# A short-convolution and MLP layer in split float32: in seven of the eight pairs of the up projection the first quadrant is turned over by a transposing DMA of half-word planes instead of by TensorE

## The reference

```python
def reference(x, ...):                      # one layer, kind 0
    h = rmsnorm(x, mix_norm)
    b_gate, c_gate, v = split(h @ w_in, 3)  # 2048 -> 3 x 2048
    y = causal_conv3(c_gate * v)            # per channel, width 3
    x = x + (b_gate * y) @ w_out
    a = relu(rmsnorm(x, mlp_norm) @ w1)     # 2048 -> 8192, the up projection
    return x + (a * a) @ w2                 # 8192 -> 2048, the down projection
```

## Time and profile before

| | us |
|---|---|
| median of three runs | 1909.17 (1907.61 to 1910.26) |
| the profiled execution | 1908.8 |
| its span, first to last instruction | 1907.1 |
| TensorE busy | 1896.7 |
| VectorE busy | 1680.6 |
| ScalarE busy | 1008.1 |
| GpSimd busy | 149.5 |
| read from and written to device memory | 431.01 MB and 93.32 MB |

### The profile page before, as it was taken

The page is one execution under the profiler, slowest core; times in us unless marked ns, Lnnn a source line. Parts: engine busy times, 40 slices in busy tenths (PEclk is TensorE's granted clock), DMA queues, the critical chain, the costliest instruction groups (busy, mean ns, idle before and its releaser), DMA issues.

```text
span 1907.1 us, 22361 instructions
## 1 busy us (share of the span) xinstructions
PE 1896.7 (99%) x8578; PEld 1573.4 (83%) x8578; DVE 1680.6 (88%) x1499; ACT 1008.1 (53%) x1082; POOL 149.5 (8%) x240
## 2 busy tenths in 40 slices
PE   9999999999999999999999999999999999999999
PEld 7888888888888888888888888888888888888887
DVE  6579899898999899988999899998998889888878
ACT  6464564545548476575665756655444343334432
POOL 1100010000011111020111201110000000000000
PEclk9999999999999999999999999999999999999999
DMA  9774768749676966876868768599888878877782
GB/s 380 250 259 127 264 205 325 233 120 330 221 199 276 353 213 205 299 276 210 332 199 307 269 216 323 198 398 399 342 329 345 353 276 314 350 312 281 295 327 116
DMA packets 120282, 525.81 MB, mean 276 GB/s; under 512 B 13040, under 2 KB 17136, under 8 KB 95216
## 3 DMA queue, kind: packets, MB, share of 16 engines
q1 hardware_dynamic: 86336, 401.64, 54.6%
q0 software_dynamic: 33696, 122.70, 21.1%
q10 hardware_dynamic: 144, 0.04, 0.0%
HBM read 431.01 MB, written 93.32 MB: 275 GB/s over the span
## 4 chain that ended last, share of the span: by engine, by line
PE 98%; DVE 1%; issue 0%; DMA 0%; ACT 0%; SPq 0%; DVEq 0%; ACTq 0%
PE pair L1226 91%; PE pair L1239 5%; PE pair L1261 3%; DMA raw<-in_turns 0%; DVE ring L938 0%; DVE raw L932 0%; DVE quads L1000 0%; DVE sum_l_mix L969 0%; ACT sum_l_mix L669 0%; DVE x L1036 0%; DVE sum L967 0%; DVE sum L969 0%; ACT ring L625 0%; DVE stage L919 0%; ACT stage L727 0%
## 5 line engine op out<-in xcount | busy, mean ns | idle before, releaser
L1226 PE MATMUL pair<-ring,act 128*128 128x512 f32 x7728 | 1768.2, 390 | 1.4 <-issue 1.4
L1226 PEld LDWEIGHTS pair<-ring,act 128*128 128x128 f32 x7728 | 1446.3, 188 | 300.7 <-issue 2.6
L625 ACT ACTIVATE ring<-raw 128x1024 fp32r<-128x1024 f32 x659 | 697.6, 1060 | 830.1 <-PE pair L1226 561.6
L938 DVE TENSOR_TENSOR ring<-raw,ring 128x1024 fp32r<-128x1024 f32 x659 | 793.4, 1220 | 170.7 <-ACT ring L625 168.1
L932 DVE TENSOR_TENSOR raw<-raw 128x1024 f32<-128x1024 f32 x312 | 367.5, 1219 | 8.2 <-issue 0.4
L492 POOL DMA_DIRECT2D spill<-stage x136 | 78.5, 618 | 474.2 <-ACT stage L727 370.8
L505 POOL DMA_DIRECT2D raw<-in_turns x56 | 50.3, 1049 | 722.4 <-DVE raw L932 721.9
L919 DVE TENSOR_TENSOR stage<-quads,stage 128x1024 fp32r<-128x1024 f32 x68 | 82.9, 1219 | 25.0 <-ACT stage L727 25.0
L1239 PE MATMUL pair<-ring,act 128*128 128x512 f32 x384 | 88.6, 393 | 2.2 <-DVE ring L849 2.2
L1239 PEld LDWEIGHTS pair<-ring,act 128*128 128x128 f32 x384 | 73.0, 190 | 17.7 <-issue 2.5
L727 ACT ACTIVATE stage<-quads 128x1024 fp32r<-128x1024 f32 x68 | 71.4, 1051 | 11.8 <-DVE quads L836 10.1
(11 more groups left out here) (103 smaller groups left out, 493.9 us busy)
## 6 DMA issues: line engine op xcount, KB each, us to landing
raw<-in_turns SPq DMA_DIRECT2D x191, 1024.0 KB, 7.1
act<-spill SPq DMA_DIRECT2D x282, 512.0 KB, 6.8
spill<-stage POOLq DMA_DIRECT2D x136, 512.0 KB, 9.3
act<-act_kept SPq DMA_DIRECT2D x68, 512.0 KB, 6.6
raw<-in_turns POOLq DMA_DIRECT2D x56, 512.0 KB, 8.7
act_kept<-act POOLq DMA_DIRECT2D x26, 512.0 KB, 9.6
x_tok<-in_x SPq DMA_DIRECT2D x4, 1024.0 KB, 15.0
x<-mixed SPq DMA_DIRECT2D x8, 512.0 KB, 16.2
```

Of the source, the lines that this page charges most:

```text
L625: nc.scalar.activation(ring[g % RING][:, 0], raw[:, raw_of(v, s), 2 * (s % 2):2 * (s % 2) + 2, :], ACT.Copy).then_inc(hi_ready, 1)
L938: nc.vector.tensor_tensor(ring[g % RING][:, 1], raw[:, raw_of(v, s), 2 * (s % 2):2 * (s % 2) + 2, :], ring[g % RING][:, 0].bitcast(F32), A ...
L1226: mm = nc.tensor.matmul(bank, stationary, moving, start=(opens and k == 0 and n == 0), stop=(closes and k == NT - 1 and n == 2))
```

## The change

In pairs 8 to 14 quadrant 0 is no longer transposed by TensorE. by_transfer(q) names these pairs.

- After the scalings of quadrant 0, at slot 13 of the odd turn, ScalarE copies the lower and the upper 16-bit halves of its words into two planes of half words (put_planes, two activations).
- SP, at the end of its work for the odd turn, waits for both and issues one transposing DMA of both planes (planes_t from planes, 512 KB).
- At slot 3 of the even turn ScalarE waits for it, copies the two turned planes back into words (two activations), waits for these, and squares the words in place (square_planes). square_quad stays for quadrants 1 to 3.
- TensorE leaves out the eight transposes ahead of slot 0. Its turn of quadrant 1 waits for no quad_ready; those of 2 and 3 wait as before.
- quad_turned counts three turns for such a pair (TURNED instead of TURNS wherever it is awaited).
- The two plane tiles take the place of S3 in acts2 (two of 4 KB), so S3 becomes a shared tile in the up projection: stored once more (keep_act) and loaded at odd turns 19 to 31. SP's load of x12, which goes to the same place for the down projection, waits until the last planes are read.

```diff
+U16 = mybir.dt.uint16
...
     TURNS.append(TURNS[-1] + (2 if _kind == GATED else 4))
+def by_transfer(q):
+
+    return KINDS[q] == UP and q < NQP - 1
+
+
+TURNED = [0]
+for _q, _kind in enumerate(KINDS):
+    TURNED.append(TURNED[-1] + (2 if _kind == GATED else 4 - by_transfer(_q)))
 RECTIFIED = [8 * sum(k in (GATE, UP) for k in KINDS[:q]) for q in range(NQP + 1)]
...
 def shared(v):
-    return (S2, L12, S3, S4, L22) if v < V_UP else (S2, S4, L22)
+    return (S2, L12, S3, S4, L22) if v < V_UP else (S2, S3, S4, L22)
 def chunk(v):
...
-KEPT = (5, 5, 0, 3)
+KEPT = (5, 5, 0, 4)
 NORM_X, NORM_M = 6, 14
...
         u_pad = at("u_pad", ACTS2 + 24 * KB, [P, NT, CW - 1 + S])
+        planes = at("planes", ACTS2 + 24 * KB, [P, 2, 2 * BW], U16)
+        planes_t = at("planes_t", ACTS2 + 28 * KB, [P, 4 * NT, P], U16)
         x_tok = [at("x_tok0", QUADS, [P, D]), at("x_tok1", QUADS + 8 * KB, [P, D]),
...
+        planes_out = sem("planes_out")
+        planes_in = sem("planes_in")
+        merged = sem("merged")
...
                         product_done(sp, v, j)
+                        if j == S3:
+                            sp.wait_ge(quad_ready, TURNS[NQP - 1])
                         q, place = {L11: ("11", x11), S1: ("21", x21), L12: ("22", x22), S3: ("12", x12)}[j]
                         load_mixed(q, place)
+                if v % 2 and by_transfer(min(v // 2, NQP - 1)):
+
+                    sp.wait_ge(planes_out, 2 * (v // 2 - UP0 + 1))
+                    sp.dma_start_transpose(planes_t[:], planes[:].rearrange("p z e -> p (z e)")).then_inc(planes_in, 16)
                 if v == V_DOWN + NC - 1:
...
                 if v == V_UP + 1:
-                    keep_act(3, S2, S4, L22)
+                    keep_act(3, S2, S3, S4, L22)
                 if v > 1:
...
             def square_quad(q, m):
-                act.wait_ge(quad_turned, TURNS[q] + m + 1)
+                act.wait_ge(quad_turned, TURNED[q] + m + 1 - by_transfer(q))
                 quads_free(act, q)
                 nc.scalar.activation(quad[("L11", "L22", "L12", "L21")[m]].rearrange("p a t -> p (a t)"),
                                      pairs[1][:].rearrange("p a t -> p (a t)"), ACT.Square).then_inc(quad_ready, 1)
+            def put_planes(q):
+
+                act.wait_ge(rectified, RECTIFIED[q] + 2)
+                words = sums_of(q)[0][:].bitcast(U16).rearrange("p t (b c z) -> p z b t c", c=P, z=2)
+                for z in range(2):
+                    nc.scalar.activation(planes[:, z].rearrange("p (b t c) -> p b t c", b=NT, t=2), words[:, z],
+                                         ACT.Copy).then_inc(planes_out, 1)
+
+            def square_planes(q):
+
+                act.wait_ge(planes_in, 16 * (q - UP0 + 1))
+                quads_free(act, q)
+                o = quad["L11"]
+                words = o.bitcast(U16).rearrange("p a (t z) -> p z (a t)", z=2)
+                for z in range(2):
+                    nc.scalar.activation(words[:, z], planes_t[:, 2 * NT * z:2 * NT * (z + 1)].rearrange("p a t -> p (a t)"),
+                                         ACT.Copy).then_inc(merged, 1)
+                act.wait_ge(merged, 2 * (q - UP0 + 1))
+                o = o.rearrange("p a t -> p (a t)")
+                nc.scalar.activation(o, o, ACT.Square).then_inc(quad_ready, 1)
+
             def by_channels():
                 return pairs[1][:].rearrange("p a (b t) -> p (a b) t", b=2)
             def take_u(q, half):
-                act.wait_ge(quad_turned, TURNS[q] + half + 1)
+                act.wait_ge(quad_turned, TURNED[q] + half + 1)
                 act.wait_ge(y_step, 2 * FORMED_U[q])
...
                             scale_tokens(q, 0)
+                            if by_transfer(q):
+                                put_planes(q)
                     if 2 <= v <= V_DOWN and v % 2 == 0:
                         kind = KINDS[q - 1]
                         if kind in (GATE, UP) and s in (2, 3, 4):
                             scale_tokens(q - 1, s - 1)
-                        if kind == UP and s in (3, 5, 6, 7):
+                        if by_transfer(q - 1) and s == 3:
+                            square_planes(q - 1)
+                        elif kind == UP and s in (3, 5, 6, 7):
                             square_quad(q - 1, {3: 0, 5: 1, 6: 2, 7: 3}[s])
...
                     pe.wait_ge(plain_copied, 4)
-                if m > 0:
+                if m > by_transfer(q):
                     pe.wait_ge(quad_ready, TURNS[q] + m)
...
                             at_slot = {3: 0, 5: 1} if KINDS[v // 2 - 1] == GATED else {0: 0, 2: 1, 4: 2, 5: 3}
-                            if s in at_slot:
+                            if s in at_slot and not (at_slot[s] == 0 and by_transfer(v // 2 - 1)):
                                 turn_quad(v // 2 - 1, at_slot[s])
...
```

More of the change, by code:

```diff
@@ L603, in direct_hi @@
                     if d == 3 and j in (L12, S3):
-                        act.wait_ge(quad_turned, TURNS[UP0])
+                        act.wait_ge(quad_turned, TURNED[UP0])
                         for m in (0, 3):
@@ L632, in place_read @@
                 if KINDS[q] != GATED or m in (0, 3):
-                    act.wait_ge(quad_turned, TURNS[q] + ({0: 1, 3: 2}[m] if KINDS[q] == GATED else m + 1))
+                    act.wait_ge(quad_turned, TURNED[q] + ({0: 1, 3: 2}[m] if KINDS[q] == GATED else m + 1 - by_transfer(q)))
                 if KINDS[q] == MIXED:
@@ L696, in take_mixed @@
             def take_mixed(q, m):
-                act.wait_ge(quad_turned, TURNS[q] + m + 1)
+                act.wait_ge(quad_turned, TURNED[q] + m + 1)
                 quads_free(act, q)
@@ L996, in gate @@
             def gate(q, m):
-                dve.wait_ge(quad_turned, TURNS[q] + m + 1)
+                dve.wait_ge(quad_turned, TURNED[q] + m + 1)
                 dve.wait_ge(y_step, 2 * FORMED_U[q])
@@ L1023, in add_product @@
                     if j == S2:
-                        dve.wait_ge(quad_turned, TURNS[NQP])
+                        dve.wait_ge(quad_turned, TURNED[NQP])
                     nc.vector.tensor_copy(o, bank).then_inc(taken, 1)
```

## The result

The changed kernel takes 1920.16 us (median of four runs, 1918.77 to 1920.95) against 1909.72 for the one before (four runs beside them): a ratio of 1.0055, 95% interval 1.0042 to 1.0067. It is slower by 10.4 us. The forecast was 1914.3, range 1905 to 1924. The direction and the range held; the loss is twice the one forecast.

The account below looks back on a forecast made before the run. TensorE was taken as the bound, at work 1896.7 of 1907.1 us. Losses of 6 x 0.80 + 0.29 = 5.1 us took the profiled 1908.8 to 1913.9, so a median of 1914.3, range 1905 to 1924.

Parts of the forecast that it names:

- Part 1: At each of seven boundaries TensorE drops one group of eight transposes: 0.87 us each, 6.1 us in all.
- Part 2: put_planes after slot 13: two half-word activations at 0.95 us each make ScalarE's slot 0 and VectorE's T1 1.55 us later.
- Part 3: The transposing transfer in SP's queue takes 6.8 us, lands 4.6 us before ScalarE wants it, and costs nothing.
- The 21 us: Extreme of the late-transfer rival: sixteen blocks transposed by DMA one after another, time near 1980; chance 0.03.
- Part 4: square_planes on ScalarE: two merging copies, a wait and an in-place square make slot 4 2.13 us later.
- Part 5: TensorE waits 1.67 us before turning quadrant 2, losing 0.80 us per boundary, 0.29 at the first; no second wait.
- Part 6: Sharing S3's activations: 8 MB more traffic and added waits in SP's queue, costed at nothing.
- B: Faster: half-word activations cost 0.62 us each, TensorE waits little, 4.4 us less, 1904.8; chance 0.10.
- C: Gain and loss cancel: TensorE's wait is 0.8 to 1.2 us, time within 1909 +- 3.8; chance 0.20.

## Why the prediction was right, and where its size was off

- **Part 1** held: 0.87 us forecast, 0.91 measured (79.79 to 78.88).
- **Part 2** held to a tenth. From ScalarE's slot 13 (882.54 in the timeline after) to its slot 0 are 4.23 us (forecast 4.3), to T1 10.04 (forecast 8.55 + 1.55), to the merging copies 15.67 (15.74). The plane copies take 1.05 us, and leaving them out moved TensorE's wait by as much as they delay slot 0. (ScalarE's busy time in the earlier trace rows is 50.09, not the 50.08 of the prediction; nothing hangs on it.)
- **Part 3** held in its result. The transfer was issued 11.3 us before it was wanted and landed after 5.2 (forecast 6.8). The rate that the Trainium skill gives ("DMA: Bandwidth & Descriptors", "Latency and other measured facts"), an estimated 2 us for 0.5 MB, is not what an issue to landing of this size shows: 5.2, and SP itself was held for a median of 3.2. The 21 us that I estimated from the Trainium skill's "VectorE: DVE Perf Modes" ("The three transpose paths") are refuted here: the table's 1309 ns are for one 128x128 block of bfloat16, and sixteen such blocks of half words in one transfer landed in 5.2 us. (The advice to prefer TensorE stands in that page's "Rules for kernel authors".)
- **Part 4** is the term that was mis-sized. I took the merging copies at 1.05 us and 0.95 from start to start; they take 1.35 (they read a dense plane and write every second half word), and from the first of them to slot 4 are 3.56 us instead of 3.0. With copies that write densely that half us went.
- **Part 5** held in mechanism: one wait, before quadrant 2, for the square of quadrant 1, at every boundary, no other. Its price by period is 80.96 - 79.79 = 1.17 us against 0.80. The 0.37 more are part 4's 0.56, less 0.07 by which ScalarE stood before the merge earlier than forecast, and less some 0.1 of a reading: the 903.15 I started from is a weight load, whose first matmul follows 0.23 later in the kernel before, but only 0.03 later behind the wait (906.95 and 906.98). What the step left out is what an idle TensorE does next: I counted the wait and took the work behind it at its usual price. At two boundaries it was dearer by 1.6 us.
- **Part 6** held for the boundaries: no change in the time with S3 shared alone. Its "nothing" left out the turn into the down projection, where the added loads come to a wait of 0.6 us.

The sum in the profile: 0.72 at the first boundary (0.29 forecast), four times 1.17, twice 2.77 with the clock: 10.9. The turns ahead of the up projection's boundaries took 1.0 us less in this execution than in the one before, as the group of transposes at 650.73 us before stands at 649.70 after; that leaves the 9.9 of the two spans. Of the 10.9, 5.1 were forecast, 2.6 are the dearer merge (with part 5's small terms) and 3.2 the clock. So the direction was forecast by its mechanism. That the time fell inside the range is owed to its width: the best guess missed half of the loss, and the clock was no term of the sum. Rivals B and C failed on the price of the half-word activation, which is that of a full word at best.

What the prediction did not ask is whether the order had to be so. It took the wait for both squares as given, where the change itself had made one of them needless.

Open: why the clock fell at two boundaries and not at the four others with the same idle time of 1.87 to 1.89 us (the first boundary has 1.48). The runs show only that the falls go with the idle time: there was none behind the waits of 1.48, 1.30 and 0.40 us, nor where the wait was filled, and there was one behind the 1.93 and one behind the 4.68.

## What to carry to other kernels

Work taken off the bound engine is won only if what stands in its place on a helper engine keeps clear of the next handover: add up the helper's work from its last anchor (the last place where it waits for the bound engine) to that handover, not its busy share (54% here). When an operand leaves a shared buffer, the waits that guarded the buffer for it, and the order they dictated, are to be looked over again; here that turned a loss of 10.4 us into a gain of 3. And each us won early moves the need for the next stage's loads forward: look who is late next.

## What the runs showed of the hardware

A 128x1024 activation on half words that writes side by side takes 1.04 us when it reads side by side and 1.05 when it reads every second one; one that reads side by side and writes every second one takes 1.35. A transposing transfer of 512 KB, SBUF to SBUF, lands 4.9 to 7.4 us after its issue in the changed kernel and holds SP's queue for 2.8 to 5.3 of them, where a load of a raw block is issued in a median of 0.33 (at most 3.0). Issued 0.4 us behind such a load, as in the kernel without plane copies, it lands after 7.4 to 9.0. An idle stretch of 1.9 us in a TensorE that is otherwise always at work was followed by the lower clock in two of six cases in the changed kernel and in two of six with the transfer doubled, for some 3.4 us.
